# Weight units loaded, split and used by halves of two chunks in a two-block float32 kernel

## The reference, cut to what matters

```python
D_MODEL, SEQ = 2048, 256
# first block
proj = rmsnorm(x, norm_a) @ w_in_a                    # 2048 x 4096
y = einsum(multiscale_causal_pool(u), w_grp_a)        # 4 groups of 512 x 512
x = x + (y * scale_a * silu(gate)) @ w_out_a          # 2048 x 2048
k, v = rmsnorm(x, norm_kv) @ w_k, ... @ w_v           # 2048 x 2048 each
q_all, gate = split(rmsnorm(x, norm_b) @ w_in_b)      # 2048 x 8192; 16 heads, 3 dilations
x = x + (merged * silu(gate)) @ w_out_b               # 2048 x 2048
x = rmsnorm(x, norm_f)
# second block, its norms modulated by vectors c @ ada_w (ada_mod)
u, v, z = split(h @ a_w_in)                           # 2048 x 12288
x = x + gate * ((u * mixed * silu(z)) @ a_w_out)      # 4096 x 2048
c_kv, k_r = split(h_kv @ kv_w_dkv)                    # 2048 x 576
kv = rms_norm(c_kv) @ kv_w_ukv                        # 512 x 4096
c_q, z = split(h @ b_w_in)                            # 2048 x 2560
q = rms_norm(c_q) @ b_w_uq                            # 512 x 3072
x = x + gate * ((attention(q, k, v) * silu(z)) @ b_w_out)  # 2048 x 2048
```

## Time and profile before

| | |
|---|---|
| median of the runs | 2352.74 us (2351.25 to 2359.21) |
| profiled execution, span | 2351.5 us |
| TensorE matmul busy | 93% |
| TensorE weight load busy | 76% |
| VectorE busy | 69% |
| ScalarE busy | 44% |
| DMA engines, mean busy share over the span | 0.59, at 220 GB/s |
| mean granted TensorE clock over the span | 0.97 of full |

### The profile page before, as it was taken

How to read it: one execution, slowest core, us unless ns; L and a number is a source line. 1 busy time by engine, 2 the same in 40 slices (tenths; PEclk the granted TensorE clock), 3 DMA queues, 4 the chain that set the end, 5 groups by cost and what they waited for, 6 DMA issues and landing times.

```text
span 2351.5 us, 29635 instructions
## 1 busy us (share of the span) xinstructions
PE 2193.1 (93%) x10034; PEld 1794.8 (76%) x10034; DVE 1632.2 (69%) x2273; ACT 1039.6 (44%) x1287; POOL 5.7 (0%) x14
## 2 busy tenths in 40 slices
PE   6999989999999999977999999999898969999998
PEld 5888767887887878765888777788787857777776
DVE  5666677776889788867777777777755565556544
ACT  4343344333344434324434444444433365767732
POOL 0000000000000000000000000000000000000000
PEclk9999999999999999988999999999999989999999
DMA  7776675777765665636577766767644535433333
GB/s 270 272 268 231 224 302 201 278 268 271 267 232 211 232 239 217 239 148 236 193 290 283 271 255 259 263 260 270 233 152 152 183 131 191 172 122 131 125 113 138
DMA packets 91005, 516.99 MB, mean 220 GB/s; under 512 B 10128, under 2 KB 10256, under 8 KB 45104
## 3 DMA queue, kind: packets, MB, share of 16 engines
q1 hardware_dynamic: 89936, 510.69, 58.7%
q10 hardware_dynamic: 544, 4.19, 0.5%
q0 software_dynamic: 448, 1.11, 0.1%
HBM read 511.76 MB, written 4.19 MB: 219 GB/s over the span
## 4 chain that ended last, share of the span: by engine, by line
PE 75%; DVE 11%; ACT 5%; issue 5%; DMA 3%; DVEq 0%; SPq 0%; ACTq 0%
PE bank L386 67%; DVE w_lo L1243 4%; DMA ada_raw<-ada_units 2%; PE bank L403 2%; ACT w_hi L781 2%; DVE ada_acc L1259 1%; PE bank L526 1%; PE bank L429 1%; PE bank L422 1%; PE bank L726 1%; PE bank L724 1%; ACT side L834 1%; DMA raw<-units 0%; DVE side L1376 0%; DVE rbuf L1365 0%
## 5 line engine op out<-in xcount | busy, mean ns | idle before, releaser
L781 ACT ACTIVATE w_hi<-raw 128x2048 fp32r<-128x2048 f32 x352 | 674.3, 1916 | 1070.6 <-PE bank L386 1027.5
L1243 DVE TENSOR_TENSOR w_lo<-raw,w_hi 128x2048 fp32r<-128x2048 f32 x352 | 806.1, 2290 | 319.4 <-ACT w_hi L781 318.5
L386 PE MATMUL bank<-w_hi,xa_hi 128*128 128x512 f32 x1952 | 781.3, 400 | 19.2 <-DVE w_lo L1243 16.1
L386 PE MATMUL bank<-w_hi,xa_lo 128*128 128x512 f32 x1952 | 763.3, 391 | 0.0
L386 PE MATMUL bank<-w_lo,xa_hi 128*128 128x512 f32 x1952 | 762.6, 391 | 0.0
L386 PEld LDWEIGHTS bank<-w_hi,xa_hi 128*128 128x128 f32 x1952 | 368.6, 189 | 108.4 <-DVE w_lo L1243 25.6
L1259 DVE SCALAR_TENSOR_TENSOR ada_acc<-ada_raw,silu_c,ada_acc 128x512 f32<-128x512 f32 x451 | 338.3, 750 | 149.9 <-DMA ada_raw<-ada_units 133.0
L386 PEld LDWEIGHTS bank<-w_hi,xa_lo 128*128 128x128 f32 x1952 | 367.7, 188 | 79.1
L386 PEld LDWEIGHTS bank<-w_lo,xa_hi 128*128 128x128 f32 x1952 | 368.7, 189 | 76.1 <-issue 2.6
L386 PE MATMUL bank<-w_hi,xb_hi 128*128 128x512 f32 (+2 forms) x864 | 342.6, 397 | 22.8 <-DVE w_lo L1243 9.8
L386 PE MATMUL bank<-w_hi,xb_lo 128*128 128x512 f32 (+2 forms) x864 | 333.0, 385 | 0.0
(11 more groups left out here) (191 smaller groups left out, 1319.7 us busy)
## 6 DMA issues: line engine op xcount, KB each, us to landing
raw<-units SPq DMA_DIRECT2D x352, 1024.0 KB, 4.8
ada_raw<-ada_units SPq DMA_DIRECT2D x258, 512.0 KB, 5.5
res<-x SPq DMA_DIRECT2D x2, 1024.0 KB, 6.4
held<-res ACTq DMA_DIRECT2D x1, 2048.0 KB, 7.3
res<-held ACTq DMA_DIRECT2D x1, 2048.0 KB, 7.4
out<-res SPq DMA_DIRECT2D x4, 512.0 KB, 7.5
side<-spatial POOLq DMA_DIRECT2D x8, 128.0 KB, 5.6
wide<-pools SPq DMA_DIRECT2D x1, 768.0 KB, 12.7
```

Source lines behind the costliest of these rows:

```text
L386: last = pe.matmul(ps[t][:, 0:cols], l, r[:, cc, :], start=c == 0 and k == 0, stop=c == CPU * units_of - 1 and k == 2)
L781: act.activation(w_hi[n0 % 2][:], raw[n0 % 2][:], ACT.Copy).then_inc(hi_done, 1)
L1243: dve.tensor_tensor(w_lo[n0 % 2][:], raw[n0 % 2][:], w_hi[n0 % 2][:], ALU.subtract).then_inc(lo_done, 1)
```

## The change

Every unit is handled as two halves of two chunks. A half has its own columns in the slot (`half * 1024` onward), its own load, its own copy to `w_hi`, its own subtraction to `w_lo`, its own wait on TensorE before its chunks, and it is given back on its own: TensorE increments `half_used` after each second chunk. `raw_in` becomes four semaphores, `lo_done` and `hi_done` count halves, and all waits on `unit_used` become waits on `half_used` with twice the count. In the units of the narrow products the copy and the subtraction cover only the columns in use (2 x 288 or 2 x 384 for each half instead of 2 x 512); the host lays these units out so that each half begins at column 1024 x half. The loads still move the whole padded unit. The order of the calls on every engine is as before.

```diff
+HALF = CPU // 2 * NB
+def width(n):
+    if UNIT0["dkv"] <= n < UNIT0["in_q"]:
+        return 288
+    if UNIT0["uq"] <= n < UNIT0["z_uq"] or (UNIT0["z_uq"] <= n < UNIT0["out_q"] and (n - UNIT0["z_uq"]) % 6 in (2, 5)):
+        return 2 * QW
+    return NB
+def half_of(a, n, i):
+    return a[n % 2][:, i * HALF:i * HALF + CPU // 2 * width(n)]
...
             def load_unit(n0, step=0, j=0):
-                if n0 >= 2:
-                    sp.wait_ge(lo_done, n0 - 1 + step * j)
                 src = units[n0] if isinstance(j, int) else units[bass.ds(n0 + step * j, 1)].rearrange("u p n -> (u p) n")
-                sp.dma_start(raw[n0 % 2][:], src).then_inc(raw_in[n0 % 2], 16)
+                for i in range(2):
+                    if n0 >= 2:
+                        sp.wait_ge(lo_done, 2 * (n0 - 2) + i + 1 + 2 * step * j)
+                    cols = slice(i * HALF, (i + 1) * HALF)
+                    sp.dma_start(raw[n0 % 2][:, cols], src[:, cols]).then_inc(raw_in[n0 % 2][i], 16)
...
-                    pe.wait_ge(lo_done, n + 1 + us * j)
-                    hi = w_hi[slot][:, 0:CPU * cols].rearrange("p (c n) -> p c n", c=CPU)
-                    lo = w_lo[slot][:, 0:CPU * cols].rearrange("p (c n) -> p c n", c=CPU)
                     for cc in range(CPU):
                         c = CPU * q + cc
+                        half, at = cc // 2, cc // 2 * HALF + cc % 2 * cols
+                        if cc % 2 == 0:
+                            pe.wait_ge(lo_done, 2 * n + half + 1 + 2 * us * j)
+                        hi, lo = (w[slot][:, at:at + cols] for w in (w_hi, w_lo))
...
-                    last.then_inc(unit_used, 1)
+                        if cc % 2:
+                            last.then_inc(half_used, 1)
...
-                act.wait_ge(raw_in[n0 % 2], 16 * (n0 // 2 + 1) + 8 * us * j)
-                if n0 >= 2:
-                    act.wait_ge(unit_used, n0 - 1 + us * j)
-                act.activation(w_hi[n0 % 2][:], raw[n0 % 2][:], ACT.Copy).then_inc(hi_done, 1)
+                for i in range(2):
+                    act.wait_ge(raw_in[n0 % 2][i], 16 * (n0 // 2 + 1) + 8 * us * j)
+                    if n0 >= 2:
+                        act.wait_ge(half_used, 2 * (n0 - 2) + i + 1 + 2 * us * j)
+                    act.activation(half_of(w_hi, n0, i), half_of(raw, n0, i), ACT.Copy).then_inc(hi_done, 1)
...
-                dve.wait_ge(hi_done, n0 + 1 + us * j)
-                dve.tensor_tensor(w_lo[n0 % 2][:], raw[n0 % 2][:], w_hi[n0 % 2][:], ALU.subtract).then_inc(lo_done, 1)
+                for i in range(2):
+                    dve.wait_ge(hi_done, 2 * n0 + i + 1 + 2 * us * j)
+                    dve.tensor_tensor(half_of(w_lo, n0, i), half_of(raw, n0, i), half_of(w_hi, n0, i), ALU.subtract)\
+                        .then_inc(lo_done, 1)
...
     def padded(u):
-        return np.pad(u, ((0, 0), (0, 0), (0, CPU * NB - u.shape[2])))
+        halves = u.reshape(len(u), P, 2, -1)
+        return np.pad(halves, ((0, 0), (0, 0), (0, 0), (0, HALF - halves.shape[3]))).reshape(len(u), P, CPU * NB)
```

More of the change, by code:

```diff
@@ L252, in build @@
         ws_in, g_in, stored = sem("ws_in"), sem("g_in"), sem("stored")
-        raw_in = [sem(f"raw_in{i}") for i in range(2)]
-        hi_done, lo_done = sem("hi_done"), sem("lo_done")
-        unit_used = sem("unit_used")
+        raw_in = [[sem(f"raw_in{i}{h}") for h in range(2)] for i in range(2)]
+        hi_done, lo_done, half_used = sem("hi_done"), sem("lo_done"), sem("half_used")
         bank_free = [sem(f"bank_free{i}") for i in range(2)]
@@ L385, in product @@
                             for k, (l, r) in enumerate(((xh, hi), (xh, lo), (xl, hi))):
-                                last = pe.matmul(ps[t][:, 0:cols], l, r[:, cc, :], start=c == 0 and k == 0,
+                                last = pe.matmul(ps[t][:, 0:cols], l, r, start=c == 0 and k == 0,
                                                  stop=c == CPU * units_of - 1 and k == 2)
-                    last.then_inc(unit_used, 1)
+                        if cc % 2:
+                            last.then_inc(half_used, 1)
                     if then is not None:
@@ L787, in after @@
                     split_hi(n0 + 2 + q, us, j)
-                act.wait_ge(unit_used, n0 + units_of + us * j)
+                act.wait_ge(half_used, 2 * (n0 + units_of) + 2 * us * j)
                 b0 = BLOCK0[name] + b
@@ L963, in set_step @@
                     b0 = BLOCK0["in_b"] + (4 if heads else 0)
-                    act.wait_ge(unit_used, UNIT0["in_b"] + 4 + (16 if heads else 0) + 16 * j)
+                    act.wait_ge(half_used, 2 * (UNIT0["in_b"] + 4 + (16 if heads else 0)) + 32 * j)
                     for t in range(NT):
@@ L1111, in take_gates @@
             def take_gates(b0, n, at, bs=0, us=0, j=0):
-                act.wait_ge(unit_used, n + us * j)
+                act.wait_ge(half_used, 2 * n + 2 * us * j)
                 for t in range(NT):
@@ L1157, in queries @@
             def queries(b0, n, freed, bs=0, us=0, gs=0, j=0):
-                act.wait_ge(unit_used, n + 1 + us * j)
+                act.wait_ge(half_used, 2 * (n + 1) + 2 * us * j)
                 act.wait_ge(turned, freed + gs * j)
@@ L1275, in after @@
                 n0 = UNIT0[name] + b * units_of
-                dve.wait_ge(unit_used, n0 + units_of + us * j)
+                dve.wait_ge(half_used, 2 * (n0 + units_of) + 2 * us * j)
                 b0 = BLOCK0[name] + b
@@ L1567, in set_step @@
                     b0 = BLOCK0["in_b"] + g + 1 + more // 4
-                    dve.wait_ge(unit_used, UNIT0["in_b"] + 4 * (g + 2) + more + 16 * j)
+                    dve.wait_ge(half_used, 2 * (UNIT0["in_b"] + 4 * (g + 2) + more) + 32 * j)
                     dve.wait_ge(turned, g0 + (6, 8, 10)[g] + 8 * j if heads else g0 + (0, 2, 4)[g])
@@ L1623, in _ @@
                         dve.wait_ge(reloaded, 16)
-                    dve.wait_ge(unit_used, n0 + q + 1)
+                    dve.wait_ge(half_used, 2 * (n0 + q + 1))
                     add_block("out_b", b)
@@ L1887, in _ @@
                     splits("out_q", b)
-                dve.wait_ge(unit_used, UNIT0["out_q"] + (7, 8, 12, 16)[b])
+                dve.wait_ge(half_used, 2 * (UNIT0["out_q"] + (7, 8, 12, 16)[b]))
                 add_gated(OUT_BLOCKS[b], SMALL0["out_q"] + b, 8 + b, b * NB)
```

## The result

The changed kernel takes 2323.8 us, the median of four runs (2316.1 to 2328.1), beside 2352.1 for the kernel before on the same chip: a ratio of 0.986 (95% interval 0.984 to 0.988). The profiled execution has a span of 2320.5 us, 31.0 less than before. Forecast were 2325 us and 27.8 us of span. The total came out as forecast, but in part by luck: several of its terms did not, their errors cancelled, and some 3.5 us of the gain are no effect of the halves (experiment 11).

A forecast was written before the change was run, and what follows sets the result against it. TensorE's matmuls cover 93% of 2351.5 us, leaving 158 us plus low-clock time. Terms 5.9 + 7.2 + 8.4 + 7.7 + 0 - 1.4 = 27.8 us gave a 2323.7 us span, forecast as 2325 us; own range 2316 to 2334, wider range 2311 to 2342.

The forecast's parts named there:

- the two terms at the ends: Stage ends: three with both splits in the path gain 5.9 us, eight with only ACT's split gain 7.2 us.
- seams are free: On TensorE, 352 more mid-unit seams, each a satisfied wait and an increment, were taken to cost nothing.
- so I take nothing: Load queue: half-megabyte pieces were read as not slower than larger ones, so half loads were priced at zero.
- The rival on loads: Smaller loads starve the slots: stages with modulation become load-bound above 1.47 times queue time; 2415 us at 1.6; chance 0.04.
- (d): Other TensorE stalls for `w_lo` outside the attention (start, `kv`, `in_v` to `in_uz`): 7.7 us gained.
- (e): First attention, three passes with six stalls of 8.9 us in all: gain 0, bounds -4 and +4.
- the surcharge on DVE: Subtracting in two halves of 1024 columns costs DVE 0.15 us more a unit than one whole subtraction.
- the passes keep their 110.4 us: Sign for the forecast: the attention's passes stay at 110.4 us; lengthening by over 1 us each would refute it.
- (c): `dkv`: 7.1 us of stalls and half of the clock's 2.5 go, 8.4 us gained (bounds 4 to 9.6).
- (f): Price paid: 0.5 us in the first attention's tail, 0.3 in each second-attention pass; 1.4 us in all.

The follow-up runs named there:

- experiment 11: shifted_code: the kernel before with 64 satisfied waits at the start of DVE's program, nothing else; 2355.1 us, ratio 0.9995.
- Experiment 7: whole_load, but ACT waits for the whole unit to be given back before copying the first half of unit n+2; ratio 0.9894.
- experiment 8: wl_seams: whole_load with a TensorE wait before every chunk and an increment behind it; 2310.3 us, ratio 0.980.
- pieces_only: The kernel before with copy and subtraction in two instructions each, but released, awaited and used as one; 2361.0 us, ratio 1.0028.
- whole_load: The change with one 1 MB load for each unit instead of two half loads; 2314.2 us, ratio 0.983.
- narrow_only: The kernel before with the narrow products' copies and subtractions cut to the columns in use, one each per unit; 2351.8 us, ratio 0.998.

## Why the prediction was right, and where it was not

**Right: the two terms at the ends.** The early return takes 0.9 us of ACT and 1.95 of both engines out of the path: 5.94 to 4.02 at the earlier trace rows, 0.86 at the end of `out_g`, 0.85 to 0.87 at the latents, keys and both `uq` units. Experiment 7 undoes it, wholly behind ACT's splits and by 1.2 of 1.98 us at the earlier trace rows. After the second `uq` unit 1.6 us came back: the turn behind it now waits 1.88 us for DVE, where it waited 0.30. That seams are free was right too (experiment 8).

**Wrong: "so I take nothing" for the smaller loads.** Rows 9 were misread. A queue that holds both sizes gave 374 GB/s at full share and one with the larger size alone 356, and I took that for the price of the smaller; but neither window held raw units in halves. Measured: 8% more queue time, 31.6 us on the kernel before, about 10 in the change. The rival on loads had the right mechanism and the wrong threshold. It reckoned with a full queue (1.47 times the time); the loss was there at a share of 0.78, where ACT's waits for loads had grown eightfold.

**Wrong: a stall's price in (d).** I added up the idle times. The stall in a pass of `in_uz`, kernel before:

```profile
1460.60 0.39 PE L386 MATMUL bank<-w_hi,xa_lo 128*128 128x512 f32 x1
1461.22 0.50 PE L386 MATMUL bank<-w_hi,xa_hi 128*128 128x512 f32 x1 [0.23 <-DVE w_lo L1243]
1461.56 0.40 PE L386 MATMUL bank<-w_lo,xa_hi 128*128 128x512 f32 x1
```

From start to start these steps are 0.62 and 0.34 us where 0.227 is the rule: 0.39 + 0.11 = 0.5 us for a stall that shows 0.23. It is 0.27 more, because the record of the matmul in front is 0.16 us longer than its step, and the step behind the stall is 0.11 longer than the rule. Each pass gained 0.65: 0.5 at this stall, 0.06 in a step that shows no idle time, the rest in hundredths. At the start 1.5 us came from the clock, low behind the stall at 42.10 in the kernel before. So (d) was worth 13.4 us with whole loads, not 7.7; half loads took some 9 of it back.

**Wrong: (e), the attention at 0.** Its 6.9 us have three parts. The first stall, before the passes, went wholly, 2.5 us in TensorE's time, of which I had booked 0.9:

```profile
650.10 0.50 PE L386 MATMUL bank<-w_hi,xa_hi 128*128 128x512 f32 x1 [2.23 <-DVE w_lo L1243]
```

A half explains 1.07 of it; DVE also comes to that split 2.2 us earlier against TensorE, and why I did not trace. The passes gained 4.1 us, but 3.5 of them are no effect of the halves: the stalls of 1.72 and 1.29 us behind the two pauses of DVE are gone because the pauses are, as in shifted_code, where nothing is split (3.5 in the same stretch), and in pieces_only, which has no early start or return (2.4, with the surcharge on it). What is left, 0.6 us, is near the 0 that I forecast: the relief (1.0 a pass) and the give-back, the new 1.28 us wait at 713.17, nearly cancel, though the surcharge on DVE was booked at 0.15 for what costs 0.07 (experiment 4). The sign "the passes keep their 110.4 us" failed: they became 108.6, mostly by the pauses.

**Too small: (c) and (f).** In `dkv` the stalls fell from 9.1 to 2.5 us, and the units at the low clock went wholly: 3.9 us, as the clock's windows of the kernel before add up, of which I had booked half of 2.5. I had counted one such unit; the one behind the stall at 1953.74 is another, and its first matmul of 0.61 us shows it. In (f) the surcharge was sized fairly (0.5 for each pass of the second attention, forecast 0.3), but the tail of the first paid 2.1 instead of 0.5, since the clock fell behind a gap of 1.78 us there that had been 1.26 (granted 0.51 from 968 to 971 us, with 9 matmuls).

In sum: with whole loads the span is 41.1 us shorter where I forecast 27.8, some 37.6 by the halves and 3.5 by the pauses, and the half loads, which I had at nothing, take 10.1 back. That 31.0 is so near 27.8 is luck: the misses of (d), (e) and the loads nearly cancel. The best version that was run is whole_load (wl_seams is the same within the interval): 40 us under the kernel before.

## What to carry to other kernels

When a slot is handed round between engines, return it in parts before you start on it in parts: here the early return was worth 16 to 18 us and the early start 4 to 10, each on top of the other. Keep the transfers whole while you cut the compute; here 1 MB loads beat 0.5 MB ones, and a queue at three quarters of its time was already the one that is late. Price an instruction or a stall from start to start, not by the length of its record or by its idle time. And look for waits that no semaphore explains before you credit a gain to your edit: here they moved 3.5 us with the place of the code.

## What was not expected of the hardware

**The same gap costs the clock or not.** After the end of `kv` TensorE idles 3.12 us in the kernel before, in narrow_only and in shifted_code. In the kernel before the granted clock stays at 1.00 from 545 to 550 us (23 matmuls); in narrow_only:

```profile
545.00:550.00 5.00, 5.00 (x13) 3.84 (x13) 1.50 (x2) 0.00 (x0) 0.00 (x0) 0.50 0.80 291
```

13 matmuls at 1.2 GHz, and TensorE 2.7 us later. In narrow_only that cost nothing in the end: the stall at 650.10 (2.23 us in the kernel before) is 0 there. Over all runs, the clock fell behind five of the eight gaps of 3.12 to 3.21 us at this place, and behind none of the four of 2.27 us that the early return leaves with whole loads. A difference of one such stretch between two executions says nothing of the edit.

**DMAs to 64 partitions** moved 178 GB/s at a share of 0.78 in `out_g`, where whole loads move 178 at 0.50: 228 GB/s at full share against 356, two thirds of the rate.
